# Spreading the routing weights of a PEER encoder with rounded-float one-hots in two parts, and ScalarE applying the high part

## What is computed

```
q = (xc @ wq).reshape(C, PEER_HEADS, 2, half)
s = jnp.einsum('thpd,hpkd->thpk', q, subkeys)
sv, si = lax.top_k(s, PEER_TOPK)
...
eid = jnp.take_along_axis(cid, fi, axis=-1)
g = jax.nn.softmax(fs, axis=-1)
a = jax.nn.gelu(jnp.einsum('tc,thkc->thk', xc, u_tab[eid]))
return jnp.einsum('thk,thkc->tc', g * a, v_tab[eid])
```

## Time and profile before

| | |
|---|---|
| median of three runs | 2104.79 us (2103.86 to 2104.86) |
| the profiled execution, whole | 2103.94 us |
| its span, first to last instruction | 2102.2 us |
| TensorE busy | 2082.1 us, 99% |
| PEld / GpSimd / VectorE / ScalarE busy | 90% / 76% / 57% / 49% |
| stretch of the 64 groups, each layer | 231.6 us |

### The profile page before, as it was taken

The page is one execution under the profiler, slowest core; times in us unless marked ns, Lnnn a source line. Parts: engine busy times, 40 slices in busy tenths (PEclk is TensorE's granted clock), DMA queues, the critical chain, the costliest instruction groups (busy, mean ns, idle before and its releaser), DMA issues.

```text
span 2102.2 us, 45874 instructions
## 1 busy us (share of the span) xinstructions
PE 2082.1 (99%) x14724; PEld 1899.4 (90%) x14724; DVE 1189.3 (57%) x2477; ACT 1037.7 (49%) x2156; POOL 1604.9 (76%) x1316
## 2 busy tenths in 40 slices
PE   8999999999999999999999999999999999999999
PEld 7888999999999888888888889999999998888887
DVE  6366469867777333333374664797777773333333
ACT  6453554454343555555564535545443435555554
POOL 6565878886767788888866668788867677888886
PEclk9999999999999999999999999999999999999999
DMA  9333545544444555555583335455434445555554
GB/s 266 121 133 117 199 155 185 183 171 141 149 142 148 173 196 190 193 196 190 197 224 129 123 121 200 161 180 182 168 142 147 144 146 181 193 195 190 194 195 150
DMA packets 102210, 357.73 MB, mean 170 GB/s; under 512 B 11424, under 2 KB 16226, under 8 KB 101636
## 3 DMA queue, kind: packets, MB, share of 16 engines
q1 hardware_dynamic: 101428, 354.45, 49.2%
q10 hardware_dynamic: 720, 2.44, 0.3%
HBM read 355.81 MB, written 1.05 MB: 170 GB/s over the span
## 4 chain that ended last, share of the span: by engine, by line
PE 59%; POOL 21%; issue 17%; POOLq 1%; ACT 1%; DVE 0%; DMA 0%; SPq 0%; DVEq 0%; ACTq 0%
PE bank L1685 33%; POOL w_lo L388 21%; PE bank L1350 8%; PE bank L1352 7%; PE bank L1354 7%; PE bank L1628 4%; POOLq L386 0%; DMA ring<-stream 0%; DVE raw_lo L827 0%; ACT w_hi L451 0%; POOLq L409 0%; ACT raw_hi L502 0%; PE bank L1709 0%; POOL e_lo L416 0%; DVE bank L920 0%
## 5 line engine op out<-in xcount | busy, mean ns | idle before, releaser
L388 POOL TENSOR_TENSOR w_lo<-ring,w_hi 128x512 fp32r<-128x512 f32 x1048 | 1404.1, 1356 | 404.9 <-ACT w_hi L451 404.6
L451 ACT ACTIVATE w_hi<-ring 128x512 fp32r<-128x512 f32 x1312 | 754.9, 621 | 673.2 <-PE bank L1354 660.3
L1350 PE MATMUL bank<-act_hi,w_hi 128*128 128x256 f32 x2688 | 777.4, 289 | 2.0 <-POOL w_lo L388 2.0
L1352 PE MATMUL bank<-act_lo,w_hi 128*128 128x256 f32 x2688 | 759.7, 283 | 0.0
L1354 PE MATMUL bank<-act_hi,w_lo 128*128 128x256 f32 x2688 | 759.2, 282 | 0.0
L1350 PEld LDWEIGHTS bank<-act_hi,w_hi 128*128 128x128 f32 x2688 | 514.0, 191 | 13.3 <-issue 6.3
L1352 PEld LDWEIGHTS bank<-act_lo,w_hi 128*128 128x128 f32 x2688 | 514.5, 191 | 1.0 <-issue 1.0
L1354 PEld LDWEIGHTS bank<-act_hi,w_lo 128*128 128x128 f32 x2688 | 514.4, 191 | 0.0
L388 DVE TENSOR_TENSOR w_lo<-ring,w_hi 128x512 fp32r<-128x512 f32 x256 | 236.4, 923 | 458.6 <-ACT w_hi L451 458.6
L1685 PE MATMUL bank<-w_hi,e_hi 128*128 128x512 f32 x1024 | 398.9, 390 | 1.7 <-DVE arena L1288 1.5
L1685 PE MATMUL bank<-w_lo,e_hi 128*128 128x512 f32 x1024 | 398.4, 389 | 0.0
(11 more groups left out here) (205 smaller groups left out, 1899.6 us busy)
## 6 DMA issues: line engine op xcount, KB each, us to landing
ring<-stream SPq DMA_DIRECT2D x656, 512.0 KB, 3.2
arena<-rpb_in SPq DMA_DIRECT2D x8, 512.0 KB, 10.3
arena<-dft_in SPq DMA_DIRECT2D x2, 1024.0 KB, 8.3
arena<-subkeys ACTq DMA_DIRECT2D x2, 1024.0 KB, 7.0
xT<-x_in SPq DMA_DIRECT2D x4, 256.0 KB, 6.5
arena<-decay_in SPq DMA_DIRECT2D x2, 512.0 KB
out<-xT SPq DMA_DIRECT2D x4, 256.0 KB, 2.5
arena<-w_in SPq DMA_DIRECT2D x2, 256.0 KB
```

What stands on the lines that cost most here:

```text
L388: eng.tensor_tensor(w_lo[:, part_, :], ring[:, tile % RING, half * HT:(half + 1) * HT], w_hi[:, part_, :].bitcast(F32), ALU.subtract).then ...
L451: nc.scalar.activation(w_hi[:, 2 * (tile % AHEAD) + half, :], ring[:, tile % RING, half * HT:(half + 1) * HT], ACT.Copy).then_inc(hi_ready ...
L1350: T.matmul(out_, weights(w_hi, tile, j), hi[:, k, :], start=start, stop=False, skip_group_check=True)
L1352: T.matmul(out_, weights(w_hi, tile, j), lo[:, k, :], start=False, stop=False, skip_group_check=True)
```

## The change

The one-hots are kept as rounded floats (`F32R`) instead of bf16. The weight is split into a rounded high part and a rest, two parts instead of three. `slotT` becomes float and holds i, j and the whole weight; the rest goes to bank 5 (`weight_lo_ps`). Per group VectorE now makes the one-hot of j straight into `weighted_hi`, the one-hot of i, and `weighted_lo` = one-hot of j times the rest: three instructions of 512 elements. ScalarE then multiplies `weighted_hi` in place by the weight, one instruction of 128 elements per token with the weight as per-partition scale (`weight_high`, four per group); its output is rounded on writing. It waits for `weighted_lo_ready`, since VectorE reads `weighted_hi` first, and TensorE's group now waits for `weighted_hi_ready` from ScalarE. A group is 8 matmuls in place of 12. The buffers `e_hi` and `e_lo` of the v phase are laid over the first half of the new buffers. The copies of the key numbers and the preparation in bf16 go.

```
@@ one_hots (VectorE)
-                    V.tensor_tensor(onehot_j[:, :, :, :], keys, over_keys(1), ALU.is_equal
-                                    ).then_inc(onehot_chain, 1)
-                    V.tensor_tensor(onehot_i[:, n % 2, :, :, :], keys, over_keys(0), ALU.is_equal)
...
-                    for a in range(PAIRS):
-                        ins = V.tensor_tensor(weighted_j[:, n % 2, a, :, :, :],
-                                              onehot_j[:, a, :, :].unsqueeze(1).to_broadcast(wide),
-                                              pair_weights(a).unsqueeze(2).to_broadcast(wide), ALU.mult)
-                    ins.then_inc(onehot_ready.sem, 1)
+                    V.tensor_tensor(weighted_hi[:, n % 2, :, :], keys, slotT[:, 1, tokens].unsqueeze(2).to_broadcast(wide),
+                                    ALU.is_equal).then_inc(onehot_j_made.sem, 1)
+                    V.tensor_tensor(onehot_i[:, n % 2, :, :], keys, slotT[:, 0, tokens].unsqueeze(2).to_broadcast(wide),
+                                    ALU.is_equal)
+                    dve.wait_ge(onehot_j_made.sem, onehot_j_made.at(l, i * RING + (n + 1)))
+                    V.tensor_tensor(weighted_lo[:, n % 2, :, :], weighted_hi[:, n % 2, :, :].bitcast(F32),
+                                    weight_lo_ps[:, tokens].unsqueeze(2).to_broadcast(wide), ALU.mult
+                                    ).then_inc(weighted_lo_ready.sem, 1)
@@ ScalarE
+                def weight_high(i, n):
+                    act.wait_ge(weighted_lo_ready.sem, weighted_lo_ready.at(l, i * RING + (n + 1)))
+                    for t in range(TOK):
+                        at = weighted_hi[:, n % 2, t, :]
+                        ins = nc.scalar.activation(at, at.bitcast(F32), ACT.Copy, scale=slotT[:, 2, bass.ds(
+                            i * (RING * TOK) + (n * TOK + t), 1)])
+                    ins.then_inc(weighted_hi_ready.sem, 1)
...
                 act.wait_ge(route_done.sem, route_done.at(l, 1))
+                weight_high(0, 0)
+                weight_high(0, 1)
                 for n in range(RING):
                     late_gelu(0, n)
+                    weight_high(0, n + 2)
@@ routing_weights (TensorE)
-                    pe.wait_ge(onehot_ready.sem, onehot_ready.at(l, i * RING + (n + 1)))
+                    pe.wait_ge(weighted_hi_ready.sem, weighted_hi_ready.at(l, i * RING + (n + 1)))
                     for t in range(TOK):
-                        for c in range(3):
-                            ins = T.matmul(bank[2 + n % 2][:, t * NK:(t + 1) * NK], onehot_i[:, n % 2, t // 2, :, t % 2],
-                                           weighted_j[:, n % 2, t // 2, c, :, t % 2], start=(c == 0), stop=(c == 2))
+                        for w_ in (weighted_hi, weighted_lo):
+                            ins = T.matmul(bank[2 + n % 2][:, t * NK:(t + 1) * NK], onehot_i[:, n % 2, t, :],
+                                           w_[:, n % 2, t, :], start=w_ is weighted_hi, stop=w_ is weighted_lo)
                     ins.then_inc(g_done.sem, 1)
```

More of the change, by code:

```diff
@@ L119, in encoder_kernel @@
         soft = sb("soft", [P, 2, 3, TT])
-        slotT = sb("slotT", [P, 5, S], BF16)
+        slotT = sb("slotT", [P, 3, S])
         table_dummy = sb("table_dummy", [P, 1])
[L122 to L125, removed]
+        onehot_i = sb("onehot_i", [P, 2, TOK, NK], F32R)
+        weighted_hi = sb("weighted_hi", [P, 2, TOK, NK], F32R)
+        weighted_lo = sb("weighted_lo", [P, 2, TOK, NK], F32R)
+        e_hi = weighted_hi[:, 0, :, :].rearrange("p t k -> p (t k)").rearrange("p (n s) -> p n s", n=AHEAD)
+        e_lo = weighted_lo[:, 0, :, :].rearrange("p t k -> p (t k)").rearrange("p (n s) -> p n s", n=AHEAD)
         bank = [ctx.enter_context(nc.psum_tensor(f"bank{i}", [P, 512], F32)) for i in range(8)]
@@ L293, in encoder_kernel @@
         route_done = sig("route_done", 1)
-        onehot_ready = sig("onehot_ready", TGROUPS)
+        onehot_j_made = sig("onehot_j_made", TGROUPS)
+        weighted_lo_ready = sig("weighted_lo_ready", TGROUPS)
+        weighted_hi_ready = sig("weighted_hi_ready", TGROUPS)
         g_done = sig("g_done", TGROUPS)
@@ L750, in act_layer @@
                 act.wait_ge(route_done.sem, route_done.at(l, 1))
+                weight_high(0, 0)
+                weight_high(0, 1)
                 for n in range(RING):
                     late_gelu(0, n)
-                with act.Fori(0, LATE // RING - 2) as i:
+                    weight_high(0, n + 2)
+                with act.Fori(0, TGROUPS // RING - 2) as i:
                     for s in range(RING):
                         late_gelu(i, RING + s)
+                        weight_high(i, RING + s + 2)
+                for n in range(TGROUPS - RING, TGROUPS):
+                    late_gelu(0, n)
+                    if n + 2 < TGROUPS:
+                        weight_high(0, n + 2)
                 for n in range(LATE - RING, LATE):
@@ L1237, in dve_layer @@
-                    if tt == 0:
-                        link(ins)
+                    V.tensor_copy(slotT[:, 0:3, cols_], src)
+                    w_top = onehot_i[:, 0, tt, :]
+                    link(V.tensor_copy(w_top, src[:, 2, :]))
+                    ins = V.tensor_tensor(weight_lo_ps[:, cols_], src[:, 2, :], w_top.bitcast(F32), ALU.subtract)
                 link(ins)
-                link(V.tensor_scalar(weight_ps.bitcast(U32), slotT[:, 2:5, :].rearrange("p c t -> p (c t)").bitcast(U32),
-                                     0, None, ALU.bitwise_or))
@@ L1265, in one_hots @@
-                    built[0] += 1
-                    dve.wait_ge(onehot_chain, built[0])
-                    wide = [P, 3, NK, 2]
-                    for a in range(PAIRS):
-                        ins = V.tensor_tensor(weighted_j[:, n % 2, a, :, :, :],
-                                              onehot_j[:, a, :, :].unsqueeze(1).to_broadcast(wide),
-                                              pair_weights(a).unsqueeze(2).to_broadcast(wide), ALU.mult)
-                    ins.then_inc(onehot_ready.sem, 1)
+                    tokens = bass.ds(i * (RING * TOK) + n * TOK, TOK)
@@ new lines, in one_hots @@
+                    wide = [P, TOK, NK]
+                    keys = keys_ps.unsqueeze(1).to_broadcast(wide)
+                    V.tensor_tensor(weighted_hi[:, n % 2, :, :], keys, slotT[:, 1, tokens].unsqueeze(2).to_broadcast(wide),
[3 more added lines that the diff above has]
+                    dve.wait_ge(onehot_j_made.sem, onehot_j_made.at(l, i * RING + (n + 1)))
```

41 lines of the change are left out of this document (3 added, 38 removed).

## The result

The changed kernel takes 2136.93 us, median of four runs (2134.68 to 2141.69), the kernel before 2104.32 (2103.76 to 2104.86): a ratio of 1.0158 with an interval of 1.014 to 1.0176. It is slower, by 32.6 us or 1.6%. The profiled execution is the longest of the four, 2141.69 us, so there are 37.7 us to account for between the spans of 2102.2 and 2139.9. First the page: span, and the busy times that answer to the earlier trace rows.

A forecast was written before the change was run, and what follows sets the result against it. TensorE was taken as the bound, busy 2082.1 of 2102.2 us. Groups +21.0 and first waits +5.8 gave +26.8 on 2104.8, so 2131.6 us, range 2127.7 to 2143.7.

The forecast's parts named there:

- the upper end: Top of the range, 2143.7 us: groups at +28.2, first waits at 6.7, and 4.0 for a lost clock.
- Price of a group: TensorE's groups: 8 float matmuls at 0.113 us make 0.90 us instead of 0.74, +21.0 us over 128 groups.
- The sign that was named: Sign of being right: on TensorE, 0.88 to 0.96 us from a group's start to the tile's.
- The pause: First group of each layer: TensorE waits 2.9 us for ScalarE's copies behind tile 59's gelu, +5.8 us in all.
- The value for the copies: ScalarE's four scaled copies of 128 elements before the first group: 1.27 us, the middle between 0.85 and 1.69.
- The clock: Half clock on TensorE after the first waits: about 2.0 us each, 4.0 for two, only in the upper end.
- a stretch at half clock behind the first wait: Sign of being wrong: TensorE running at half clock after its wait at a layer's first group.
- Steady rounds: Every later round: 3.78 us on TensorE, with VectorE and ScalarE fitting inside and no new wait, cost 0.
- The hidden load: Rival for TensorE's groups: rounded-float loads overlap, a group costs 0.49 us, total 2079 us; chance 0.12, plus 0.02 for coming out even.
- VectorE as the bound: Rival for every round: VectorE's new operations take 0.92 us each, its round 4.0 us, total 2159 us; chance 0.07.
- The dear rate: Rival for TensorE's groups: rounded floats with few columns cost 0.222 us each, a group 1.78, total 2243 us; chance 0.11.
- the change does what it says: Rival on the matmul count, set aside: one-hots of i already shared by two matmuls; 12 loads a group spoke against it.

The follow-up runs named there:

- e3_cols64: The changed kernel with 64 moving columns instead of 128 in each of the group's matmuls, half of each routing matrix left out: 2136.5 us.
- e6_no_act: The changed kernel without ScalarE's products; TensorE's group waits for `weighted_lo` instead: 2130.83 us.
- e4_load64: The changed kernel with 64 stationary columns instead of 128 in each of the group's matmuls, half of each routing matrix left out: 2092.0 us.
- e5_bf16_two: The kernel before with the weight in two bf16 parts instead of three, 8 bf16 matmuls per group: 2075.45 us, ratio 0.9866.
- e7_pad64: The changed kernel with 64 unused bytes ahead of `onehot_i`, so `e_hi` and `e_lo` begin at a multiple of 128 bytes: 2135.90 us.

## Why the prediction was right, and where it was not

The sign, the bound and the size were right: 2131.6 us forecast, 2136.93 measured, inside the forecast's own range of 2127.7 to 2143.7. But of +32.6 us the sum had +26.8, and not for the reason that its range allowed for. Two terms were missing (the v phase, 6.7, and in the median some 1.6 for the clock) and one was too large (the groups, by 2.4). That the total stayed inside is in part luck: the upper end had been drawn for dearer groups and a lost clock, and it took in a v phase that nobody had thought of.

*Price of a group.* Right in kind, a little high: 0.113 us per matmul was forecast and 0.111 measured, and the 8 x 0.113 counted each of the eight alike, where the boundary with the tile is cheaper: 0.84 us from the first matmul to the tile's plus 0.05 behind it. 0.885 instead of 0.90 is +18.6 instead of +21.0. The sign that was named, 0.88 to 0.96 us from a group's start to the tile's, was missed by as much: it is 0.84, with the tile's second matmul 0.17 behind its first instead of 0.12. Reading the price from loads with one moving column held; 64 moving columns in `e3_cols64` are the test of it.

*The pause.* Right: 2.9 us forecast, 2.83 measured, with the causes in the order given. The value for the copies, 1.27 us for four, came out at 1.26; it was the middle between 0.85 and 1.69, chosen without a reason for the middle, so that it fits so well is luck.

*The clock.* This step failed. The text said that the idle time was a third of that at the start of the span and left the drop out of the sum; in the profiled execution it came in both layers. The step argued from one long idle time that a short one would be harmless, which that row could not show. One of the forecast's own signs of being wrong, a stretch at half clock behind the first wait, did appear. The estimate, 2.0 us for one, was also low: 3.05 measured, since the spell is 6.8 us, not 4.65. As an upper end it was in the range; as a term of the sum it deserved a chance of its own. It comes in some executions and not in others, so neither zero nor 6.1 is the answer for the median, which has some 1.6.

*The v phase.* Missed altogether, 6.7 us, and no rival held it. That `e_hi` and `e_lo` are laid over the new buffers stands in the description of the change, and the sum has no term for it. It moves no instruction, but it moves addresses, and the address of these two has a price.

*Steady rounds.* Right: round 3.765 forecast as 3.78, VectorE's operations 0.60 us apart, ScalarE idle for 1.14 us, GpSimd untouched; `e6_no_act` shows the cost of zero.

*The rivals.* The hidden load needed 0.087 us or less per matmul; the distance is 0.111, and `e3_cols64` and `e4_load64` say why. VectorE as the bound needed 0.92 us per operation; L1262, the one that reads what was just written, starts 0.59 us behind its neighbour. The dear rate of 0.222 us is excluded by the same timeline. That the change does what it says shows in the counts: 512 matmuls less. Among bf16 matmuls the cost does go nearly with their count, as `e5_bf16_two` shows: a group of 0.52 us for eight, where 8/12 of 0.74 is 0.49.

## What to carry to other kernels

Price a matmul with few moving columns by its stationary load and type, not by its count: here eight float ones cost more than twelve bf16 ones, and the one-column matmul elsewhere in the trace told it in advance. When a change hands an in-order engine a new last step before a phase, look at what it stands behind in the first round, and add a possible half-clock stretch to the wait. When a change moves buffers, compare the addresses of matrix operands, here their offset from a multiple of 128 bytes, in parts of the program that it doesn't touch.

## What the hardware showed that was not expected

- Where the buffers of the float stationary operand (`e_hi` and `e_lo`) begin 64 bytes past a multiple of 128, the matmuls that use them follow each other more slowly: 351.5 us against 348.2 for the v phase in the changed kernel, and 358.2 in the kernel before with the same offset. The five kernels looked at that have them at a multiple of 128, in three different places, all gave 348.2 to 348.3. The load records stay at 188 ns. What decides between 3.3 and 10.0 us is open.
- After a wait of 2.7 us TensorE ran at the 1.2 GHz level for 6.8 us, though it was busy throughout; after the same wait in the other layer of another execution it did not. A wait of 1.87 us in `e7_pad64` was followed by a half-clock stretch too, one of 1.3 us in `e6_no_act` was not.
